# Layer 0's attention rebuilt as one interleaved walk, with its first keys and queries loaded ahead

## What is computed

```python
def diff_attn_core(q, k, v, lam, scale):
    s = jnp.einsum('bqhjd,bkhjd->bhjqk', q.astype(F32), k.astype(F32)) * scale
    p = jax.nn.softmax(s, axis=-1)
    pd = p[:, :, 0] - lam * p[:, :, 1]
    return jnp.einsum('bhqk,bkhe->bqhe', pd, v.astype(F32)).astype(v.dtype)
...
        o = rmsnorm(o, subln_g) * (1.0 - lam_init)
```

## Time and profile before

| | us |
|---|---|
| median of 3 runs | 3508.03 (3506.77 to 3509.52) |
| the profiled execution's own time | 3507.99 |
| its span in the trace | 3506.2 |
| mean granted clock of TensorE, as a share of 2.4 GHz | 0.962 |

### The profile page before, as it was taken

How to read it: one execution, slowest core, us unless ns; L and a number is a source line. 1 busy time by engine, 2 the same in 40 slices (tenths; PEclk the granted TensorE clock), 3 DMA queues, 4 the chain that set the end, 5 groups by cost and what they waited for, 6 DMA issues and landing times. The chain is left out here.

```text
span 3506.2 us, 42803 instructions
## 1 busy us (share of the span) xinstructions
PE 3180.8 (91%) x14958; PEld 2594.5 (74%) x14958; DVE 1840.3 (52%) x2494; ACT 1029.1 (29%) x1843; POOL 1542.0 (44%) x1123
## 2 busy tenths in 40 slices
PE   7995777499999999999997869999997999999999
PEld 6774555388888888888775647777775788888887
DVE  5683666554454444444535756676775633333333
ACT  3322676213000000000233436666662300000000
POOL 3682554064232232222432217777777632332332
PEclk9997899699999999999998969999998999999999
DMA  6566320132212122111113782323223211111111
GB/s 224 158 192 183 102 76 1 54 118 79 67 60 66 60 66 66 60 60 60 42 67 127 222 254 56 83 55 83 55 55 122 79 51 42 52 48 43 49 48 64
DMA packets 165311, 302.48 MB, mean 86 GB/s; under 512 B 53344, under 2 KB 103264, under 8 KB 164576
## 3 DMA queue, kind: packets, MB, share of 16 engines
q1 hardware_dynamic: 153696, 259.32, 24.8%
q10 hardware_dynamic: 11520, 41.95, 4.0%
HBM read 235.69 MB, written 65.54 MB: 86 GB/s over the span
## 5 line engine op out<-in xcount | busy, mean ns | idle before, releaser
L127 POOL TENSOR_TENSOR small<-ident 128x1 f32<-128x1 f32 x170 | 53.3, 313 | 1164.9 <-PE ps L163 665.1
L1348 POOL TENSOR_TENSOR a_pl<-a_p,a_ph 128x512 fp32r<-128x512 f32 x320 | 430.5, 1367 | 177.3 <-ACT a_p L1322 177.1
L163 PE MATMUL ps<-hidden,whi 128*128 128x512 f32 (+1 forms) x1760 | 499.9, 369 | 8.6 <-POOL wlo L138 5.1
L2014 DVE SCALAR_TENSOR_TENSOR residual<-ps,mod,residual 128x512 f32<-128x512 f32 (+1 forms) x440 | 302.8, 696 | 375.0 <-PE ps L163 374.9
L138 POOL TENSOR_TENSOR wlo<-raw,whi 128x1024 fp32r<-128x1024 f32 x170 | 441.0, 2594 | 14.2
L163 PE MATMUL ps<-mixed_hi,whi 128*128 128x512 f32 (+1 forms) x1200 | 426.9, 356 | 14.9 <-POOL wlo L138 10.9
L163 PE MATMUL ps<-mixed_lo,whi 128*128 128x512 f32 (+1 forms) x1200 | 425.8, 355 | 0.0
L163 PE MATMUL ps<-mixed_hi,wlo 128*128 128x512 f32 (+1 forms) x1200 | 425.4, 355 | 0.0
L163 PEld LDWEIGHTS ps<-hidden,whi 128*128 128x128 f32 x1760 | 319.6, 189 | 65.1 <-POOL wlo L138 5.2
L1825 ACT ACTIVATE hidden<-gated 128x512 fp32r<-128x512 f32 (+1 forms) x110 | 64.8, 589 | 998.6 <-DVE gated L2003 998.6
L2003 DVE TENSOR_TENSOR gated<-gated,ps 128x512 f32<-128x512 f32 (+1 forms) x110 | 69.9, 635 | 510.3 <-PE ps L163 494.0
(11 more groups left out here) (307 smaller groups left out, 6203.2 us busy)
## 6 DMA issues: line engine op xcount, KB each, us to landing
raw<-in_w_ffn SPq DMA_DIRECT2D x132, 512.0 KB, 3.6
l_vraw<-in_mod_t ACTq DMA_DIRECT2D x56, 512.0 KB, 3.7
raw<-in_w_out SPq DMA_DIRECT2D x32, 512.0 KB, 3.8
a_k<-scratch_k SPq DMA_DIRECT2D x32, 480.0 KB, 6.7
f_vraw<-in_mod_t ACTq DMA_DIRECT2D x24, 512.0 KB, 4.2
a_q<-scratch_q SPq DMA_DIRECT2D x32, 384.0 KB, 5.6
a_k<-scratch_k SPq DMA_DIRECT2D x32, 320.0 KB, 10.8
a_v<-scratch_v SPq DMA_DIRECT2D x32, 320.0 KB, 5.2
```

The costliest lines, as they stand in the source:

```text
L127: e.nc.gpsimd.tensor_tensor(e.spare[:, 0:1], e.ident[:, 0:1], e.ident[:, 0:1], ALU.mult)
L163: last = nc.tensor.matmul(out, a, b, start=at == 0, stop=at == n - 1)
L1348: nc.gpsimd.tensor_tensor(pl[:, kk % 2, c], p[:, kk % 2, c], ph[:, kk % 2, c].bitcast(F32), ALU.subtract).then_inc(s["pl"], 1)
L2014: last = nc.vector.scalar_tensor_tensor(h[:, m, a:a + w], e.ps[:, o:o + w], e.mod[:, g, c:c + 1], h[:, m, a:a + w], ALU.mult, ALU.add)
```

## The change

Front. Of the last tiles, Q 7 to 9 come earlier and the U tiles after them, so the last two turns end with U tile 9. After U tile 7 SP waits for the stored keys and loads head 0's keys (8 DMAs of 320 KB) into SBUF, after U tile 9 it waits for the last q store and loads the queries (4 DMAs). Two of U's weight pieces go to other slots and steps.

Attention. One exponential of 1280 columns for each map (PSUM holds map 0's latent scores, both context scores and map 1's latent scores side by side). Map 0 isn't scaled any more: DVE makes the factor -lambda * sum0 / sum1, POOL scales map 1 by it (in two parts, 1024 and 256 columns) and adds it to map 0. What is left out, the division by sum0, cancels in the norm, whose epsilon is multiplied by sum0 squared. Units are two key tiles by two query tiles: four transposes, ACT's high and DVE's low part of 512 columns, six matmuls of 256 columns; 21 for each head. The norm is done inside the walk for each head: POOL squares, ten one-column matmuls sum ("s"), ACT's root, DVE's reciprocal, then five blocks of 256 columns ("b": spread on PE, product on DVE, high part on ACT, low part on POOL). The stage `norm` is gone. The walk has 50 periods n: units a and b of a pair of query tiles are in odd n, c, d and e in the next even n; a unit's value matmuls are two units behind its transposes.

Pool mixer: it loads the residual, and waits for it at its end. Heads1: the second value half has a bank of its own, one that the queries use before.

```diff
+def attention0(e, qs, ks, vs, P, p1, pth, ptl, o_sb, sq, tmp, ahi, alo):
...
+    N, LAG, PT, RING_P = 10 * HEADS0, 2, 3, 6
...
+        M0, CB, M1, TB, OB = 0, 2 * BANK, 2 * BANK + 2 * CTX, 5 * BANK, 7 * BANK
...
+        def units_in(n):
+            out = []
+            if n % 2 and n >= 3 and (n - 3) // 2 < PAIR_COUNT:
+                J = (n - 3) // 2
+                out = list(range(first_unit[J], first_unit[J] + (2 if J % 5 < 4 else 1)))
+            if n % 2 == 0 and n >= 4 and (n - 4) // 2 < PAIR_COUNT and (n - 4) // 2 % 5 < 4:
+                J = (n - 4) // 2
+                out = list(range(first_unit[J] + 2, first_unit[J] + 5))
+            return out
+
+        def extras_in(n):
+
+            h, x = divmod(n - 13, 10)
+            if not 0 <= h < HEADS0:
+                return []
+            if x == 0:
+                return [("s", h)]
+            if h == HEADS0 - 1:
+                return [("b", h, p) for p in range(5)] if x == 2 else []
+            return [("b", h, p) for p, at in enumerate((2, 4, 6, 8, 9)) if at == x]
+
+        def values_in(n):
+
+            us = units_in(n)
+            if n % 10 == 1 and n >= 11:
+                return [us[0] - 2], [us[0] - 1]
+            if n % 10 == 2 and n >= 12:
+                return [first_unit[(n // 10) * 5] - 1], []
+            out = []
+            for u in us:
+                v = u - LAG
+                out.append(v if v >= 0 and v // 21 == u // 21 else None)
+            return out[:1], out[1:]
+
...
+                def context(n):
+                    h, q = divmod(n, 10)
+                    if q >= 8:
+                        pe.wait_ge(s["e0"], n)
+                    pe.wait_ge(s["e1"], n)
...
+                def latent(n, m):
+                    h, q = divmod(n, 10)
+                    pe.wait_ge(s[f"e{m}"], n)
...
+                def bank_free(x):
+
+                    if turn_index[x] < 2:
+                        return
+                    y = turn_order[turn_index[x] - 2]
+                    if y[0] == "u":
+                        pe.wait_ge(s["lo"], y[1] + 1)
+                    elif y[0] == "s":
+                        pe.wait_ge(s["vv"], y[1] + 1)
+                    else:
+                        pe.wait_ge(s["tmp"], 5 * y[1] + y[2] + 1)
+
+                def turn(u):
+                    J, k = pair_of(u)
+                    pe.wait_ge(s["comb"], 2 * J + 2)
+                    bank_free(("u", u))
...
+                def value(u):
+                    J, k = pair_of(u)
+                    h = J // 5
...
+                    pe.wait_ge(s["lo"], u + 1)
...
+                        nc.tensor.matmul(o, vh, ph, start=k == 0 and x == 0, stop=False)
+                        nc.tensor.matmul(o, vh, pl, start=False, stop=False)
+                        last = nc.tensor.matmul(o, vl, ph, start=False, stop=final)
+                    last.then_inc(s["pv"], 1)
...
+                for n in range(PERIODS):
+                    h, q = divmod(n, 10)
+                    us = units_in(n)
+                    va, vb = values_in(n)
+                    if n < N and q == 0:
+                        arrived(h)
+                    if n < N and q < 8:
+                        latent(n, 0)
+                    for u in us[:1]:
+                        turn(u)
+                    for v in va:
+                        if v is not None:
+                            value(v)
+                    if n < N:
+                        context(n)
+                        if q < 8:
+                            latent(n, 1)
+                    for x in range(max(len(us[1:]), len(vb))):
+                        for u in us[1 + x:2 + x]:
+                            turn(u)
+                        for v in vb[x:x + 1]:
+                            if v is not None:
+                                value(v)
+                    for x in extras_in(n):
+                        extra(x)
...
+                def exps(n, m):
+                    h, q = divmod(n, 10)
+                    a = 0 if q < 8 else LAT
+                    if m == 0:
+                        if n >= RING_P:
+                            act.wait_ge(s["turn"], last_turn(n - RING_P) + 1)
+                        act.wait_ge(s["n0"], n + 1)
+                        src, dst = e.ps[:, M0 + a:M0 + T], P[:, n % RING_P, a:T]
+                        total = s0[:, h % 2, q:q + 1]
+                    else:
+                        if n >= 2:
+                            act.wait_ge(s["comb"], n - 1)
+                        if q < 8:
+                            act.wait_ge(s["n1"], lat_before(n) + 1)
+                        src, dst = e.ps[:, M1 - CTX:M1 + LAT - a], p1[n % 2][:, 0:T - a]
+                        total = s1[:, n % 2:n % 2 + 1]
+                    nc.scalar.activation(dst, src, ACT.Exp, bias=nb[:, n % 2, m:m + 1], accum_out=total).then_inc(s[f"e{m}"], 1)
...
+                for n in range(PERIODS + 1):
+                    before = units_in(n - 1)
+                    for J in copies_at(n - 1):
+                        copy_out(J)
+                    for x in extras_in(n - 2):
+                        if x[0] == "s":
+                            act.wait_ge(s["vv"], x[1] + 1)
+                            nc.scalar.activation(sd[:], vv[:], ACT.Sqrt).then_inc(s["sd"], 1)
+                    for u in before[1:2]:
+                        high(u)
+                    if 1 <= n <= N:
+                        exps(n - 1, 1)
+                    for u in before[2:]:
+                        high(u)
+                    for u in units_in(n)[:1]:
+                        high(u)
+                    for x in extras_in(n - 2):
+                        if x[0] == "b":
+                            normed(*x[1:])
+                    if n < N:
+                        exps(n, 0)
...
+                def factor(n):
+                    x = n % 2
+                    dve.wait_ge(s["e1"], n + 1)
+                    dve.wait_ge(s["e0"], n + 1)
+                    nc.vector.reciprocal(r1[:, x:x + 1], s1[:, x:x + 1]).then_inc(s["rec"], 1)
...
+                for n in range(PERIODS + 1):
+                    lat = n < N and n % 10 < 8
+                    before = units_in(n - 1)
+                    if lat:
+                        top(n, 0)
+                    for u in before[1:2]:
+                        low(u)
+                    if n < N:
+                        context_top(n)
+                    if lat:
+                        negative(n, 0)
+                    if 1 <= n <= N:
+                        factor(n - 1)
+                    if lat:
+                        top(n, 1)
+                        negative(n, 1)
+                    for u in before[2:]:
+                        low(u)
+                    for x in extras_in(n - 1):
+                        extra(x)
+                    for x in extras_in(n - 2):
+                        if x[0] == "s":
+                            dve.wait_ge(s["sd"], x[1] + 1)
+                            nc.vector.reciprocal(rd[:], sd[:]).then_inc(s["rd"], 1)
+                    for u in units_in(n)[:1]:
+                        low(u)
...
+                def combine(n):
+                    q, slot = n % 10, n % RING_P
+                    pool.wait_ge(s["cc"], n + 1)
+                    parts = (((0, LAT, CTX), (LAT, T, 0)) if q < 8 else ((LAT, T, 0),))
+                    for y, (a, b, at) in enumerate(parts):
+                        w = b - a
+                        nc.gpsimd.tensor_scalar(p1[n % 2][:, at:at + w], p1[n % 2][:, at:at + w], cc[:, n % 2:n % 2 + 1], 1.0, ALU.mult,
+                                                ALU.mult).then_inc(s["mul"], 1)
+                    pool.wait_ge(s["mul"], lat_before(n) + n + len(parts))
+                    for y, (a, b, at) in enumerate(parts):
+                        last = nc.gpsimd.tensor_tensor(P[:, slot, a:b], P[:, slot, a:b], p1[n % 2][:, at:at + b - a], ALU.add)
+                    last.then_inc(s["comb"], 1)
+
+                def square(J):
+                    h, p = divmod(J, 5)
+                    pool.wait_ge(s["out"], J + 1)
+                    if h:
+                        pool.wait_ge(s["turn"], turn_index["s", h - 1] + 1)
+                    o = o_sb[:, h % 2, 256 * p:256 * p + 256]
+                    nc.gpsimd.tensor_tensor(sq[:, 256 * p:256 * p + 256], o, o, ALU.mult).then_inc(s["sq"], 1)
+
+                def normed_low(h, p):
+                    x = 5 * h + p
+                    pool.wait_ge(s["nhi"], x + 1)
+                    nc.gpsimd.tensor_tensor(alo[:, h, 256 * p:256 * p + 256], tmp[:, x % 2, :], ahi[:, h, 256 * p:256 * p + 256].bitcast(F32),
+                                            ALU.subtract).then_inc(s["nlo"], 1)
+
+                for n in range(PERIODS + 1):
+                    if 1 <= n <= N:
+                        combine(n - 1)
+                    for J in copies_at(n - 1):
+                        square(J)
```

(33 more changed lines are left out.)

610 lines of the change are left out of this document (210 added, 400 removed).

## The result

The changed kernel takes 3590.07 us (median of four runs, 3577.73 to 3591.25) against 3507.4 us for the kernel before (3506.5 to 3509.52): ratio 1.0227, 95% interval 1.0204 to 1.025. The forecast was 3564 with a range of 3492 to 3638.

The account below looks back on a forecast made before the run. A chain of waits in the attention, no engine full, was taken to set the pace. Attention +53, prefetch -19, residual +1, heads1 -5 make +30; with +26 for the clock, 3508 + 30 + 26 = 3564 us, range 3492 to 3638.

Parts of the forecast that it names:

- the walk: Step-by-step addition of the attention's periods from row prices at full clock: fortieth period starts 355.7 us after the first.
- Heads1: Layer 1's projections: another bank cuts PE's wait for the low value half, -5 us, between 0 and -12.
- The tail: End of the attention, after the fortieth period starts (last units, square, s, root, five b pieces): about 26 us.
- The "s" step: Each head's attention period where the "s" piece waits for POOL's square: 14.75 us at full clock, the next 10.85.
- this chain: Attention: PE and DVE take turns, two periods take 17.8 us; ACT's table for the root was put beside it.
- The prefetch: Ahead of the attention: loading head 0's keys and queries early nearly removes PE's wait, -19 us, between -12 and -20.
- rival (4): Prefetch fails: query loads are held on SP and the front's end waits with them; 3583 us, chance 0.06.
- Residual: Pool mixer: residual loads queue behind U's loads and land shortly before the stage's end; +1 us, between 0 and +5.
- The clock: Attention: PE's granted clock taken as 0.88, +6.5 us for each head, +26 in all, bounds 0 and +125.
- 383 + 26: Attention with the norm inside: 383 us at full clock against 329.9 before, plus 26 for the lower clock.
- (1): Faster: PE and DVE don't alternate, the attention keeps today's pace, a head near 67 us; 3451 us, chance 0.17.
- (3): Attention: PE falls to 1.2 GHz and stays there; 3538 + 110 = 3648 us, chance 0.12.

Follow-up runs that it names:

- the new lists: Changed kernel with the engines' lists reordered and rings of five instead of three for halves of turned tiles: 3421.88 us, 0.9755 of the kernel before.
- The experiment on the clock: Changed kernel with eight extra matmuls on PE ahead of its waits in nearly every period from the eighth on: 3589.14 us.
- the three runs with the same attention: Changed kernel with the prefetch undone (3604.37 us), one bank for layer 1's values (3591.12 us), or the prefetch in another order (3595.29 us).

## Why the prediction was right, and where it wasn't

- **Sign and size.** 3590 for 3564, inside the range; the mechanism, PE and VectorE taking turns, is there. The steps of the latent periods without pieces were forecast, for the full clock, at 8.55, 8.45 and 8.4 and came at 9.24, 8.19 and 8.12; those with a "b" piece at 10.0 and 10.7 and came at 11.76, 11.35 and 11.96; 7.0 and 7.9 came as 6.62 and 7.61. Thirteen periods: 97.8 forecast, 102.2 measured. The tail: 26 forecast, 23.7 measured (714.19 to 737.84). One small slip of the walk: its value(e) ends at 5.6, where its own prices add up to 5.44.
- **The cause inside the mechanism.** The walk gives the two reasons side by side, the low half last on VectorE and the turn and values ahead of the scores on PE. It is the second that costs. The low half moved alone gave nothing that one run can show; the scores moved alone gave 107 us. The prediction took this order as given and did not ask what the order of the kernel before, scores first, would make of the new units.
- **The "s" step and the one behind it,** the terms that failed most: 14.75 + 10.85 = 25.6 forecast, 18.45 + 16.12 = 34.6 measured. PE runs these steps mostly at half clock (0.57 from 422 to 460 us): the twenty one-column records took 4.40 us for 2.29. The wait of the "s" matmuls for POOL's square is there as forecast (9.1 us in the four heads). And the turn behind them needs the bank that the mean frees, 4.02 us of waiting, of which 2.31 are the epsilon term, an operation that the walk did not price.
- **The norm's cost.** "ACT's table for the root and back is beside this chain" held here, where the chain was slow; in the new lists, with steps of 5.6, the steps with the tables are the longest of the head.
- **POOL** did not bind, as said: of the waits of PE's turns 14.4 us are for it, 104.4 for VectorE (75.0 for low halves, 29.4 for the norm's product and mean).
- **The prefetch:** -19 forecast, -8.8 measured (-6.7 to -10.9 in the runs with the same prefetch), less than even the bound of 12, and rival (4) has its gap (18.24 us ahead of the first score). The step that failed is the work of the queues. The issue times were counted, not the bytes: eight key transfers put 2.6 MB ahead of the front's last stores. The seven stores behind them landed after 9.3 to 10.5 us where they took 2.2 to 3.1, and the last turned tile waited 11.84 us for them:

```profile
303.54 0.60 ACT L2534 ACTIVATE f_oh<-ps 128x512 fp32r<-128x512 f32 x1 [11.84 <-DMA scratch_q<-f_ol]
...
310.33 1.06 SPq L2234 DMA_DIRECT2D scratch_u<-f_tmp  x2
317.85 0.32 SPq L264 DMA_DIRECT2D a_v<-scratch_v  x1
```

At the end the same happens once more: the last two stores of U stand behind the four query transfers, land 6.4 to 6.7 us after their issue at 310.33, and the front ends with them, at 317.85.

- **Residual:** +1 forecast, 0 measured. **Heads1:** -5 forecast, -8.3 measured; 3 to 8 us of it are the second bank's.
- **The clock:** 0.88 taken, midway between two rows of 0.77 and 0.99; 0.85, 0.75 and 0.76 measured. A head was forecast at 104 us with it and took 109.4 and 110.5. The experiment on the clock does not tell how much of this is the clock's, so that the size of this term stays open. The Trainium skill's rule (TensorE: Matmul & The Clock Gate, "A second HAM failure mode: psum-queue depth-cycling") spoke for the upper part of this term; the trace agrees so far as the clock swings between both levels within a head, 0.50 from 422 to 446 us and 1.00 from 498 to 506.
- **The sum.** In the profiled execution the stage takes 419.8 for 383 + 26, 10.8 more; the prefetch gave 10.2 less; the residual, heads1 and the rest are 7.2 better (1 + 3.3 + 2.9): 13.8 over the forecast. The other three executions of the changed kernel are 12 to 14 us longer and have no trace of their own; the three runs with the same attention have stages of 426.5 to 432.0, 17 to 23 over the forecast. So the nearness of 3564 to the measured time owes something to luck: the terms of the stage and of the prefetch were both too small, and layer 1 came out better.
- **Rivals.** (1) asked for the alternation not to form. It formed, but its argument, that about 50 us of work for each engine would fit a head of 67, was sound: with the lists in another order and longer rings a head takes 61. (3) was priced at +110 for the clock where the term itself is bounded by +125, without a reason given; nothing measured bears on it. (4) was priced at 3583, nearer to the measured 3590 than the forecast, and it was right on the prefetch.

## What to carry to other kernels

Where several engines pass tiles in a ring, walk the period twice: once in the order written, once with the producer of the scarce input (here the score matmuls that VectorE waits for) first in its list. If the second walk is shorter, it is the list and not the change that costs. Reordering one engine's list cost nothing and was worth 107 us; two slots more in a ring were worth 55 in the new lists.

A prefetch is not free because its issue is early: count its bytes against the stores that the stage before must still land. The clock was a follower here: it came back by itself, from 0.75 to 0.91, when PE's list was put in order.

## What the runs showed of the hardware that was not expected

- A VectorE operation on 128x10 elements with both operands in SBUF took 2.31 us when it started just behind the start of POOL's addition of 1024 columns, and ended 0.02 to 0.03 us behind that addition:

```profile
L492 DVE SCALAR_TENSOR_TENSOR a_eps<-a_sum x4: 159/1238/2308, 444.7 to 730.4; 128x10 f32<-128x10 f32 x4
```

Ten of the traces here (all but the one with the term on ScalarE) have it 40 times after the change. All 13 instances that started inside such an addition ended with it, whether 1.84 or 2.38 us were left of it. The other 27 took 0.16 to 0.28 us: five that started up to 0.12 us ahead of such an addition, and those beside POOL's scaling of 256 columns or beside an idle POOL. The mean, as small and with one operand in PSUM, took 0.17 at 664.53, inside an addition. So VectorE's reading of two SBUF operands waited for POOL's addition here as a whole.

- PE with 480 matmuls in a window instead of 349, the extra ones ahead of its waits, had its granted clock raised from 0.75 to 0.89, and the kernel did not get faster by it.
